# Fifteen phase edges of a three-block fp32 layer stack: clears by ranges, loads in another order, a shared join

## Reference

```python
# block 1
z = rmsnorm(x) @ w_in                  # -> spatial unit (u, v, gate), gated linear attention (q, k, v, gate, rank-16 decay)
x = x + rmsnorm(concat(sgu, gla) @ w_out)
# block 2
u = x @ w_in                           # -> bidirectional mLSTM (4 heads), window attention with sink (8 heads, 2 KV heads)
x = layernorm(ALPHA * x + concat(mlstm, gqa) @ w_out)
x = layernorm(ALPHA * x + (silu(x @ w_g) * (x @ w_u)) @ w_ffn_out
              + sigmoid(x @ w_ple_gate) * (p @ w_ple_proj))       # p: 1024 x 256
# block 3
x = layernorm(x)
u = x @ w_in                           # -> bidirectional gated delta rule (4 heads), neighbourhood attention (8 heads)
x = layernorm(ALPHA * x + concat(delta, na) @ w_out)
x = layernorm(ALPHA * x + act(x @ w1 + b1) @ w2 + b2)
```

## Time and profile before

| what | value |
|---|---|
| runs | 4214.26, 4220.49, 4230.47 us |
| median | 4220.49 us |
| profiled execution, its own time | 4226.41 us |
| its span, first to last instruction | 4225.1 us |
| mean granted PE clock | 0.955 of full |
| busy: PE, DVE, ACT, POOL | 3864.9, 1677.2, 1338.0, 412.2 us |
| phase edges (start of the first clear, us) | 153.2, 404.8, 724.5, 913.0, 1018.9, 1276.8, 1418.3, 1521.4, 2393.8, 2505.8, 3032.0, 3352.0, 3456.3, 4189.9, 4223.9 |
| clears at them | 50, 25, 31, 10, 46, 32, 34, 16, 39, 51, 42, 73, 10, 28, 21 |

### The profile page before, as it was taken

One profiled execution on the slowest core, in us unless ns is written; L12 is line 12 of the kernel. 1 busy time (PEld: TensorE's weight loads), 2 busy tenths in 40 slices (PEclk: granted clock), 3 DMA queues, 4 the chain that ended last, 5 costly groups with the idle time before them and its releaser, 6 DMA issues. The chain is left out here.

```text
span 4225.1 us, 53099 instructions
## 1 busy us (share of the span) xinstructions
PE 3864.9 (91%) x20940; PEld 3048.1 (72%) x20940; DVE 1677.2 (40%) x2765; ACT 1338.0 (32%) x2309; POOL 412.2 (10%) x288
## 2 busy tenths in 40 slices
PE   8998999988998879999999979998587789999998
PEld 4776887866666658888888656666477667888886
DVE  3343322224565543222222534555256544333234
ACT  4354222223565341111111345555423322111112
POOL 2000000020004030000000320000243130000001
PEclk8999999999999999999999999999789899999999
DMA  2011011121112111111111121111201011111111
GB/s 82 30 31 55 26 45 50 45 79 33 30 37 91 35 46 45 50 45 50 46 48 46 42 56 43 50 50 51 81 27 37 27 40 40 49 50 45 50 50 55
DMA packets 85582, 199.42 MB, mean 47 GB/s; under 512 B 18696, under 2 KB 20168, under 8 KB 85272
## 3 DMA queue, kind: packets, MB, share of 16 engines
q1 hardware_dynamic: 85400, 196.96, 15.0%
HBM read 183.75 MB, written 15.14 MB: 47 GB/s over the span
## 5 line engine op out<-in xcount | busy, mean ns | idle before, releaser
L396 ACT ACTIVATE b_ffn_wh<-b_ffn_raw 128x1024 fp32r<-128x1024 f32 (+1 forms) x140 | 146.1, 1043 | 611.2 <-PE b_ffn_space L382 611.2
L381 PE MATMUL b_ffn_space<-b2f_x_lo,b_ffn_wh 128*128 128x512 f32 x800 | 316.0, 395 | 0.0
L380 PE MATMUL b_ffn_space<-b2f_x_hi,b_ffn_wh 128*128 128x512 f32 x800 | 311.3, 389 | 1.0 <-DVE b_ffn_wl L448 1.0
L382 PE MATMUL b_ffn_space<-b2f_x_hi,b_ffn_wl 128*128 128x512 f32 x800 | 310.4, 388 | 0.0
L448 DVE TENSOR_TENSOR b_ffn_wl<-b_ffn_raw,b_ffn_wh 128x1024 fp32r<-128x1024 f32 (+1 forms) x140 | 182.6, 1305 | 230.2 <-ACT b_ffn_wh L396 199.3
L380 PE MATMUL b_ffn_space<-b3f_hidden_hi,b_ffn_wh 128*128 128x512 f32 x512 | 199.2, 389 | 0.0
L382 PE MATMUL b_ffn_space<-b3f_hidden_hi,b_ffn_wl 128*128 128x512 f32 x512 | 199.2, 389 | 0.0
L381 PE MATMUL b_ffn_space<-b3f_hidden_lo,b_ffn_wh 128*128 128x512 f32 x512 | 199.2, 389 | 0.0
L381 PE MATMUL b_ffn_space<-b3f_x_lo,b_ffn_wh 128*128 128x512 f32 x480 | 189.3, 394 | 0.0
L380 PE MATMUL b_ffn_space<-b3f_x_hi,b_ffn_wh 128*128 128x512 f32 x480 | 187.3, 390 | 0.5 <-DVE b_ffn_wl L448 0.5
L382 PE MATMUL b_ffn_space<-b3f_x_hi,b_ffn_wl 128*128 128x512 f32 x480 | 186.9, 389 | 0.0
(11 more groups left out here) (620 smaller groups left out, 9012.6 us busy)
## 6 DMA issues: line engine op xcount, KB each, us to landing
b_ffn_raw<-w SPq DMA_DIRECT2D x64, 512.0 KB, 3.5
b_ffn_raw<-w_ffn SPq DMA_DIRECT2D x44, 512.0 KB, 3.6
all_x<-xT SPq DMA_DIRECT2D x16, 512.0 KB, 7.2
b_out_raw<-w_out SPq DMA_DIRECT2D x16, 512.0 KB, 3.6
b_ffn_raw<-w_ffo SPq DMA_DIRECT2D x16, 512.0 KB, 3.6
g_heads<-na_done SPq DMA_DIRECT2D x16, 512.0 KB, 2.9
na_feed_raw<-w_gqkv SPq DMA_DIRECT2D x24, 256.0 KB, 3.2
b_head_raw<-w_bv SPq DMA_DIRECT2D x16, 256.0 KB, 7.2
```

The lines of the kernel that those rows point to most:

```text
L380: nc.tensor.matmul(acc[i][:, c], wh[i][:, wk], xh[:, c], start=(k == 0), stop=False)
L381: nc.tensor.matmul(acc[i][:, c], wh[i][:, wk], xl[:, c], start=False, stop=False)
L382: last = nc.tensor.matmul(acc[i][:, c], wl[i][:, wk], xh[:, c], start=False, stop=(k == st.KT - 1))
L396: nc.scalar.activation(wh[i][:, 0:st.KT * P], raw[i][:, 0:st.KT * P], ACT.Copy).then_inc(hi_done, 1)
```

## The change

- Semaphores are cleared by ranges: the phase's numbers are sorted, and each run of consecutive ones is one clear.
- Loads are issued in another order. The norm tables (-30 to -41) now stand ahead of the first weight tiles (-45 to -20, and the heads' -40) and of the first head's x; the sink and the attention biases of `gqa`, the norm tables, mask and position tables of `na` (-50 to between -5 and 0) behind the first weights. In `na` the additions to the position tables are planned at 9 and 10 instead of negative times. In `delta` head 0's keys come first, then a gate row, values, the other gate row, queries, `levels` and end rows; the wait for end rows moves to 20.
- `b2_ffn`: pT is loaded, rounded and lowered in two halves, lowered by DVE instead of POOL; the opening's four chains of 24 matmuls are yielded step by step, so that they merge with the embedding's; planned times shift (`AT` 7.0 to 7.5, `EACH` 2.9 to 3.4).
- First head: `paired=False`; POOL adds no squares, PE picks each squared block, 16 groups of eight matmuls instead of 8; the root is planned 1.8 earlier after its last square.
- End of `na`: five of eight blocks are joined by DVE, three by POOL.
- `delta`: the first head's first mask on DVE instead of POOL; its exponentials are planned at 0, 2.5, 5.5 and 6.6.

```diff
-        for sem in self.sems:
-            self.nc.sync.sem_clear(sem)
+        numbers = sorted(sem.num for sem in self.sems)
+        while numbers:
+            run = [n for i, n in enumerate(numbers) if n == numbers[0] + i]
+            self.nc.sync.sem_clear(range(run[0], run[-1] + 1))
+            numbers = numbers[len(run):]
...
-                        yield -45.0
+                        yield -20.0 + i
                         sp.dma_start(raw[i][:, 0:stages[0].KT * P], stages[0].w[i]).then_inc(w_landed[i], 16)
...
+                def opening(half, i):
+                    st, c = stages[0], slice(half * HALF, (half + 1) * HALF)
+                    for k in range(st.KT):
+                        yield lead.opens(half, i, k)
+                        if half == 0 and k == 0:
+                            pe.wait_ge(lo_done, i + 1)
+                            pe.wait_ge(taken, i + 1)
+                            if i:
+                                lead.second_free(pe)
+                        lead.wait(pe, half, k)
+                        xh, xl = st.rhs(k)
+                        wk = slice(k * P, (k + 1) * P)
+                        nc.tensor.matmul(acc[i][:, c], wh[i][:, wk], xh[:, c], start=(k == 0), stop=False)
+                        nc.tensor.matmul(acc[i][:, c], wh[i][:, wk], xl[:, c], start=False, stop=False)
+                        last = nc.tensor.matmul(acc[i][:, c], wl[i][:, wk], xh[:, c], start=False, stop=(k == st.KT - 1))
+                    if half:
+                        last.then_inc(acc_ready, 1)
+
                 if lead is not None:
-                    weave(*lead.tensor(pe))
-                    st = stages[0]
-                    for half in range(2):
-                        for i in range(2):
...
+                    weave(*lead.tensor(pe), *(opening(half, i) for half in range(2) for i in range(2)))
...
     def root_at(self, h):
-        return self.squares_at(h, DT - 1) + 3.4
+        return self.squares_at(h, DT - 1) + (3.4 if self.paired is not None else 1.6)
...
     def picking(self, pe):
-        for m in range(DT):
+        each = 2 if self.paired is not None else 1
+        for m in range(2 * DT // each):
...
     def loads(sp):
-        yield -30.0
+        yield -41.0
         sp.dma_start(pick[:].rearrange("p a b -> p (a b)"), consts["pick_rows"]).then_inc(landed, 16)
...
+    def opens(self, half, i, k):
+        if i and self.first is not None:
+            return self.first.end() + 0.7 * (DT * half + k)
+        return self.split.time(half, k if self.first is not None else DT * i) + 2.9 + 0.01 * k
...
-        self.first, self.weights_at, self.wait = first, 10.0, self.split.wait
+        self.first, self.weights_at, self.wait = first, 12.6, self.split.wait
...
-    KT, AT, EACH = 2, 7.0, 2.9
+    KT, AT, EACH = 2, 7.5, 3.4
...
     def loads(self, sp):
-        yield -44.0
-        sp.dma_start(self.base[:, 0:2, :], self.source).then_inc(self.p_landed, 16)
+        for h in range(2):
+            yield -49.0
+            c = slice(h * HALF, (h + 1) * HALF)
+            sp.dma_start(self.base[:, 0:2, c], self.source[:, :, c]).then_inc(self.p_landed[h], 16)
...
+    def lowering_inputs(self, ve):
+        for h in range(2):
+            yield 6.1 + 2.3 * h
+            ve.wait_ge(self.p_high, h + 1)
+            c = slice(h * HALF, (h + 1) * HALF)
+            self.nc.vector.tensor_tensor(self.pair.lo[:, 0:2, c], self.base[:, 0:2, c], self.pair.hi[:, 0:2, c], ALU.subtract).then_inc(self.p_low, 1)
...
-                    yield -50.0
+                    yield -5.0
                     sp.dma_start(sink[:], d["a_sink"].broadcast_to([P, 8])).then_inc(sink_landed, 16)
...
                     yield -50.0
+                    head(0, 1)
+                    gate_row(0, 0)
+                    head(0, 2)
+                    gate_row(0, 1)
+                    head(0, 0)
                     sp.dma_start(levels[:].rearrange("p d l c -> p (d l c)"), d["g_levels"]).then_inc(levels_landed, 16)
...
-                        for dr in range(2):
+                        for dr in range(0 if h else 1, 2):
                             yield HEAD * h - 8.0 + 2.5 * dr
...
-                                yield HEAD * h - 3.0 + 2.2 * half + 1.1 * dr
+                                yield HEAD * h - 3.0 + 2.2 * half + 1.1 * dr if h else (5.5 + 1.1 * dr if half else 2.5 * dr)
...
+                    nc.vector.tensor_tensor(pt[0][:, 0], pt[0][:, 0], outside[:, 0:1, :].broadcast_to([P, DT, P]), ALU.add).then_inc(masked[0], 1)
+                    yield 20.0
                     for dr in range(2):
                         ve.wait_ge(end_landed[dr], 16)
...
-                    yield -50.0
+                    yield -5.0
                     sp.dma_start(outside[:], d["na_columns"]).then_inc(outside_landed, 16)
                     for b in range(HEADS):
-                        yield begin + (DT * b - 9) * SPACE
+                        yield max(begin + (DT * b - 9) * SPACE, -4.0)
...
-                join_blocks(nc.gpsimd, (pair, x), range(DT))
+                join_blocks(nc.gpsimd, (pair, x), range(5, DT))
...
-                            yield begin + (DT * b - 4 + j) * SPACE
+                            yield max(begin + (DT * b - 4 + j) * SPACE, 9.0 + j)
...
+                def joining():
+                    for k in range(5):
+                        yield plan[-1][0] + plan[-1][1] + 2.0 + 1.3 * k
+                        if k == 0:
+                            ve.wait_ge(feed.acc_ready[1], len(kinds))
+                        join_blocks(nc.vector, (pair, x), (k,))
```

More of the change, by code:

```diff
@@ L770, with __init__ @@
     STEP, SQUARES = 0.62, 6
-    def __init__(self, nc, ph, name, consts, tables, banks, x, out, g, b, eps, centre_at, scale_at, scale_step, sums=None, free=(), sq=None):
+    def __init__(self, nc, ph, name, consts, tables, banks, x, out, g, b, eps, centre_at, scale_at, scale_step, sums=None, free=(), sq=None, paired=True):
         self.nc, self.consts, self.x, self.out, self.g, self.b, self.eps = nc, consts, x, out, g, b, eps
@@ L780, in __init__ @@
         self.meaned = [ph.sem(f"{name}_meaned{h}") for h in range(2)]
-        self.centred, self.squared, self.paired, self.summed = (ph.sem(f"{name}_{what}") for what in ("centred", "squared", "paired", "summed"))
+        self.centred, self.squared, self.summed = (ph.sem(f"{name}_{what}") for what in ("centred", "squared", "summed"))
+        self.paired = ph.sem(f"{name}_paired") if paired else None
         self.rooted, self.inverted, self.spreaded = ([ph.sem(f"{name}_{what}{h}") for h in range(2)] for what in ("rooted", "inverted", "spreaded"))
@@ L970, in gpsimd @@
     def gpsimd(self, pool):
-        return [self.norm.pairing(pool), self.split.lowering(pool, self.norm.nc.gpsimd, 1)] + ([self.first.lowering(pool)] if self.first is not None else [])
+        return ([self.norm.pairing(pool)] if self.norm.paired is not None else []) + [self.split.lowering(pool, self.norm.nc.gpsimd, 1)] + ([self.first.lowering(pool)] if self.first is not None else [])
     def tensor(self, pe):
@@ L980, in vector @@
     def vector(self, ve):
-        return [self.norm.centring(ve), self.norm.inverses(ve), self.norm.scaling(ve), self.split.lowering(ve, self.norm.nc.vector, 0)]
+        return [self.norm.centring(ve), self.norm.inverses(ve), self.norm.scaling(ve), self.split.lowering(ve, self.norm.nc.vector, 0)] + (
+            [self.first.lowering_inputs(ve)] if self.first is not None else [])
 class Embedding:
-    KT, AT, EACH = 2, 7.0, 2.9
+    KT, AT, EACH = 2, 7.5, 3.4
     def __init__(self, nc, ph, bank, inside, w, source, base, pair):
@@ L1077, in __init__ @@
     def __init__(self, nc, ph, consts, tables, banks, x, out, g, source):
-        super().__init__(nc, ph, "pre", consts, tables, (None,) + banks, x, out, g, None, 1e-6, (3.3, 13.6), (13.0, 22.5), 0.72)
+        super().__init__(nc, ph, "pre", consts, tables, (None,) + banks, x, out, g, None, 1e-6, (3.3, 13.6), (11.6, 21.4), 0.72, paired=False)
         self.source = source
@@ L1128, in first_head @@
         v_ready, v_taken = ph.sem("v_ready"), ph.sem("v_taken")
-        split = Halving(nc, ph, "split", h, pair, (13.8, 23.3), 0.72, norm.scaled, read=gate_read)
+        split = Halving(nc, ph, "split", h, pair, (12.4, 22.2), 0.72, norm.scaled, read=gate_read)
         w3 = d["w_bv"].rearrange("p (t n) -> p t n", t=DT)
         ba = cols["b_a2"]
-        begin = [16.0] + [28.0 + 6.5 * n for n in range(DT - 1)] + [74.0 + TILE * n for n in range(DT)]
+        begin = [14.6] + [26.6 + 6.5 * n for n in range(DT - 1)] + [74.0 + TILE * n for n in range(DT)]
         length = [12.0] + [6.5] * (DT - 1) + [TILE] * DT
@@ L1166, in _ @@
             def _(pool):
-                weave(norm.pairing(pool), split.lowering(pool, nc.gpsimd, 1))
+                weave(split.lowering(pool, nc.gpsimd, 1))
             @block.tensor
@@ L3084, in masking @@
                     for h in range(G_H):
```

(4 more changed lines are left out.)

100 lines of the change are left out of this document (50 added, 50 removed).

## The result

The changed kernel takes 4167.23 us (median of four runs, 4165.01 to 4179.09) against 4222.39 for the kernel before beside it (4214.26 to 4230.47): a ratio of 0.9874, with a 95% interval of 0.9854 to 0.9894. That is 55.2 us less; 60.5 was forecast, 7 us from the predicted 4160 and inside the range. The profiled execution took 4168.8, its span is 4167.4 and its mean PE clock 0.963 of full.

What follows compares the result with a forecast made beforehand. Phase bodies were taken as mostly PE-bound, with holes at phase edges where the change works. Terms 28.0 + 12.0 + 12.1 + 1.0 + 9 - 1.6 = 60.5 off 4226.4 gave 4165.9, predicted as a 4160 median, range 4138 to 4186.

Steps and rivals of the forecast that it cites:

- the first head's root: First head: with POOL's pairing gone, the root, ahead of four weight casts on ACT, was to come 2 us earlier.
- Clears, 28.0: All phase edges: a range clear costs as much as one single, 0.062 us; 28.9 gained less 0.9 for mlstm.
- Loads, 12.0: Reordered loads: gqa 1.7, na 8.9, third block's head 0.4 and feed-forward 1.0, second block's head 0.
- b2_ffn's opening, 12.1: Second block's feed-forward: picks near 1527, 10.7 earlier (0.9 of it clears), plus 2.3 from weaving; bounds 7 and 16.
- the step by which the woven chains fill half of the idle and a little more (+2.3): Second block's feed-forward: chains woven between the embedding's steps fill over half of PE's 4.0 us idle after first picks.
- The gains are given back in the body: Rival: na and delta give back 21 us if their ends hang on ACT or DVE; 4181 us, chance 0.10.
- Join, 1.0: End of na: DVE and POOL take turns on block additions, phase ends 0.7 to 1 earlier; ends 0.6 and 7.
- The rival without contention: End of na: DVE's and POOL's additions don't slow each other; 6 us more gained, 4154 us, chance 0.12.
- Delta, 9: Delta's opening: keys load first, DVE's first product 14.1 after the start; gain 9 us beside clears, bounds 5 and 11.
- The third rival: Na and delta give back 21 us inside their bodies, for 4181 us; chance 0.10.
- First head, a loss of 1.6: First head: unpaired picks cost 3.6 in the second half, root 2 earlier; from a loss of 4 to a gain of 1.
- The rival that the new openings would bring half-clock stretches with PE full: New openings: earlier but thinner work brings 10 us stretches at 1.2 GHz, nine making it slower, 4250 us; chance 0.02.

Runs made afterwards that it cites:

- second pair: One more profile each of the kernel before and the changed kernel, both without edit; spans 4216.9 and 4166.4 us.
- POOL's join: Changed kernel with all eight block additions at the end of na back on POOL; 4170.48 us, ratio 0.9867.
- the late one: Changed kernel with DVE's five block additions placed behind the norm's last scaling, POOL's three as they are; 4168.84 us, ratio 0.9869.
- first pair: The first profiles of the kernel before and the changed kernel; profiled executions 4226.4 and 4168.8 us, span 57.7 us shorter.
- only-clears: Kernel before with only the clears by ranges added; 4193.91 us, ratio 0.9933.
- the stopped kernel: Changed kernel with all joins on DVE and PE made to wait between b2_ffn's woven opening and the loop; 4163.13 us, ratio 0.9866.
- the unwoven one: Changed kernel with the feed-forward openings' first four chains behind the lead's work, not woven with it; 4179.85 us, ratio 0.9894.

## Why the prediction was near, point by point

The forecast of 60.5 against a measured 55.2 is right in its large terms. Three smaller steps failed: the second block's opening, the join and the first head's root; and the first head's half-clock stretches hide the last in a single pair of profiles.

- **Clears, 28.0.** Measured alone 28.6. One range takes little more than a single did (0.039 us in the median, 0.108 at most, against 0.062 from one single to the next). The 0.9 taken off for `mlstm` was wrong, for 2.2 came out there; `b3_ln` gave less.
- **Loads, 12.0.** The step that carried most held: na's first matmul 4.25 us after SP's first load (4.5 predicted), and the order is worth 8.95 at PE's start (8.9 predicted) and 10.3 in the phase of a single profile. In gqa it is 4.1 (4.65 predicted). In `b2_head` the picks come 9.9 earlier and the phase is 0.2 shorter, as said, since the root hangs on a weight cast.
- **b2_ffn's opening, 12.1: the term that was mis-sized.** Of the 13.0 with its clears 8.4 came out in the opening. The picks did come earlier (7.1 into the phase, 6 predicted), but the step by which the woven chains fill half of the idle and a little more (+2.3) failed: from first pick to loop it is 64.0 us, 63.1 before. The first window shows why: from 1503 to 1514 PE had only 8.5 us of work in 11 and the clock was 0.53, so nearly all at 1.2 GHz. PE's busy time to the loop rose from 58.3 to 60.5. Before the change only the first 2.9 us behind the first pick were at 1.2 GHz. The other profiles bear it out: in three of the nine with a woven opening and no stop the clock was full for good from 11.4 us into the phase, and it is 62.1 from first pick to loop; in the other six it was from 16.3 to 18.3, and it is 63.6 to 64.0. Then the loop at 233.3 ns instead of 228.9 took 4.6 more in some 1050 matmuls. In the second pair the opening gained 10.0, and the loop went from 231.1 to 233.3 and took 2.3. No rival had this; "The gains are given back in the body" is its form, in another phase than I named and by another mechanism.
- **Join, 1.0.** It was 0.5 of a loss. The engines took turns as forecast and DVE's additions ended as forecast (12.21 for 12.7), but the norm's 5.1 us from reciprocal to last scaling became 6.8: PE, which had had nothing to do since its last product, ran at 1.2 GHz from 2978.3 to 2988.0, and eight of its spreading matmuls took 2.04 us. In the kernels whose norm was done or nearly done when the clock fell (POOL's join, the late one, DVE's) it was 5.0 to 5.2 again. The rival without contention falls, since DVE's five took twice their own time.
- **Delta, 9.** First product 14.7 into the phase (14.1 predicted). The opening gained 10.6 with its clears; the phase gained 7.4 in the first pair, 9.4 in the second, and 9.1 by the means of the two profiles before and the ten with the new opening. The first profile's body behind that product, 297.9 us, is one of the longest of the ten (293.1 to 298.3; with the old opening 292.7 to 295.1 in four). The third rival, in which delta and na give back 21, isn't borne out; a give-back of 1 or 2 can't be told from the scatter.
- **First head, a loss of 1.6.** The matmuls are 2.8 us later at 60 us (4.3 in the second pair; the bound was 4). The cost of the picks in the second half was forecast right (3.6, measured 3.4 to 3.6); the 2 us that the root was to gain failed, for the picks of the first half are one run on PE and the root waits for its end. The first profile's 7.0 of gain is the missing half-clock stretch.
- **The clock.** The rival that the new openings would bring half-clock stretches with PE full isn't borne out: the mean clock rose from 0.955 to 0.963.

By terms: 28.6 clears, 12 to 13 loads, 2.9 for `b2_ffn` beside its clears (8.4 - 0.9 - 4.6; 6.9 in the second pair), -0.5 join, 8 to 8.5 delta, -2.8 head (-4.3 in the second pair). With the numbers of either pair that makes 48 to 52, against 55.2 by the medians and 57.7 and 50.5 by the pairs' spans. The rest, 3 to 7 us by the medians, isn't assigned to a term: `sgu` alone shortened by 3.3 and 3.2 in the two pairs where the 25 clears ahead of it explain 1.6. Single phases differ between executions by as much.

## What to carry to other kernels

At a phase edge, what counts is the time from the barrier to the first load that PE needs; tables and masks that are needed later go behind it, and one range clear does the work of fifty. An opening's gain has to be followed to the phase's end, by the start of the n-th matmul in both traces, because a PE that is "100% busy" at full clock can still be 2% slower. An addition of two SBUF tiles shared between DVE and POOL isn't shared work: here DVE alone, fitted between the norm's steps, was faster than both together (na 5.3 us shorter by the traces; the runs 4161.1 against 4170.5 with POOL alone and 4168.8 with DVE's part late on the same chip, and against 4167.2 and 4168.3 of the changed kernel on others).

## What was not expected of the hardware

- PE's matmuls of 512 columns in the second block's feed-forward, in a full stretch at full clock, come every 228.9, 231.1 or 233.3 ns, and keep the distance over a thousand matmuls. The kernel before showed 228.9 once and 231.1 once, only-clears and the stopped kernel 231.1, the unwoven one 228.9, and all nine profiles with a woven opening and no stop 233.3, in the opening's last chain as in the loop. The kernel with only the clears had 233.3 in its unwoven opening too, and 231.1 behind a stop of 0.92 us. So the weave doesn't make the distance: it removes the stop at which it could change, and the opening's own is handed on. A stop isn't the only place of change: where the input becomes `b2f_hidden`, all fourteen profiles go to 226.7 ns without one. What sets the distance was not found.
- A PE that is full runs at half clock for 0 to 20.5 us somewhere between 76 and 100 us of the first head, from execution to execution, in both orders of the head.
- While DVE and POOL both have additions of two SBUF tiles queued, they take turns, and each slows: 3.35 to 3.38 us instead of 1.15 to 1.23 on DVE, 3.31 to 3.38 instead of 2.33 to 2.35 on POOL.
